# A chunked RWKV-7 scan with one multiplication by the inverse, and rotary queries projected once

## The reference, cut to what matters

```
# RWKV-7, per head of 64 (8 heads), token by token
sa    = einsum('bhvk,bhk->bhv', state, a_t)
state = state * w_t + sa[..., None] * b_t + v_t[..., None] * k_t
y_t   = einsum('bhvk,bhk->bhv', state, r_t)

# MLA: 8 heads of 64 plain and 32 rotary columns
q      = rms_norm(c_q, q_norm) @ w_uq
q_rope = [x1 * cos - x2 * sin, x2 * cos + x1 * sin]     # halves of the 32
```

## Time and profile before

| | us |
|---|---|
| median of 3 runs (1507.62 to 1509.68) | 1509.52 |
| the profiled execution | 1508.86 |
| its span in the trace | 1507.1 |

### The profile page before, as it was taken

How to read it: one execution, slowest core, us unless ns; L and a number is a source line. 1 busy time by engine, 2 the same in 40 slices (tenths; PEclk the granted TensorE clock), 3 DMA queues, 4 the chain that set the end, 5 groups by cost and what they waited for, 6 DMA issues and landing times.

```text
span 1507.1 us, 24905 instructions
## 1 busy us (share of the span) xinstructions
PE 1475.0 (98%) x9685; PEld 1218.0 (81%) x9685; DVE 1043.1 (69%) x1626; ACT 683.4 (45%) x1232; POOL 132.5 (9%) x163
## 2 busy tenths in 40 slices
PE   6999999999999999999999999999999999999998
PEld 5987888777777888887788888888888888888887
DVE  6566764578687582679865489777777757777785
ACT  7555664244433213756313246444444433333453
POOL 1013320000010001364000020000000000000000
PEclk9999999999999999999999999999999999999999
DMA  5031002722222536204446115444443699889754
GB/s 193 15 80 43 16 16 63 225 68 71 83 73 62 170 126 150 90 4 137 130 163 240 54 58 175 152 153 154 150 149 136 229 332 326 277 281 301 270 180 151
DMA packets 181115, 216.53 MB, mean 144 GB/s; under 512 B 28789, under 2 KB 115186, under 8 KB 180242
## 3 DMA queue, kind: packets, MB, share of 16 engines
q1 hardware_dynamic: 180942, 215.11, 43.5%
q10 hardware_dynamic: 68, 0.02, 0.0%
HBM read 156.20 MB, written 56.92 MB: 141 GB/s over the span
## 4 chain that ended last, share of the span: by engine, by line
PE 84%; DVE 8%; ACT 4%; issue 2%; DMA 2%; SPq 0%; ACTq 0%; DVEq 0%
PE bank L3113 20%; PE bank L3511 20%; PE bank L3575 13%; PE bank L3476 5%; PE bank L3417 4%; PE bank L3011 3%; PE bank L3023 2%; PE bank L3038 2%; PE bank L2900 2%; PE bank L2967 2%; PE bank L3048 2%; DVE down_raw L2715 1%; DVE hacc L2755 1%; PE bank L3606 1%; PE bank L2931 1%
## 5 line engine op out<-in xcount | busy, mean ns | idle before, releaser
L3113 PE MATMUL bank<-uT_hi,w_hi 128*128 128x512 f32 x432 | 170.8, 395 | 0.0
L3113 PE MATMUL bank<-uT_hi,w_lo 128*128 128x512 f32 x432 | 168.2, 389 | 0.0
L3113 PE MATMUL bank<-uT_lo,w_hi 128*128 128x512 f32 x432 | 168.2, 389 | 0.0
L3575 PE MATMUL bank<-mg_lo,mg_hi 128*128 128x512 f32 x576 | 134.8, 390 | 0.6 <-DVE mg_hi L2722 0.6
L3575 PEld LDWEIGHTS bank<-mg_lo,mg_hi 128*128 128x128 f32 x576 | 107.9, 188 | 24.2 <-DVE mg_hi L2722 1.9
L3575 PE MATMUL bank<-yh,mg_lo 128*128 128x512 f32 x384 | 118.2, 389 | 0.0
L1419 ACT ACTIVATE zbuf<-bank 128x512 f32<-128x512 f32 x54 | 32.2, 599 | 173.2 <-PE bank L3113 168.9
L1786 ACT ACTIVATE f<-f 128x512 f32<-128x512 f32 x64 | 40.5, 632 | 131.6 <-DVE f L2680 69.7
L3113 PEld LDWEIGHTS bank<-uT_hi,w_hi 128*128 128x128 f32 x432 | 81.1, 188 | 21.7 <-issue 5.2
L3113 PEld LDWEIGHTS bank<-uT_hi,w_lo 128*128 128x128 f32 x432 | 81.1, 188 | 17.4 <-issue 1.0
L3113 PEld LDWEIGHTS bank<-uT_lo,w_hi 128*128 128x128 f32 x432 | 81.1, 188 | 17.1
(11 more groups left out here) (510 smaller groups left out, 3759.2 us busy)
## 6 DMA issues: line engine op xcount, KB each, us to landing
down_raw<-in_w_ff_down SPq DMA_DIRECT2D x80, 512.0 KB, 4.9
down_raw<-f_spill SPq DMA_DIRECT2D x56, 512.0 KB, 4.8
f_spill<-x SPq DMA_DIRECT2D x80, 256.0 KB, 2.9
w_raw<-in_w_in SPq DMA_DIRECT2D x28, 512.0 KB, 4.2
sgate<-gate_spill SPq DMA_DIRECT2D x16, 512.0 KB, 4.2
up_a<-in_w_ff_up SPq DMA_DIRECT2D x16, 512.0 KB, 4.9
up_b<-in_w_ff_up SPq DMA_DIRECT2D x16, 512.0 KB, 4.1
f_spill<-f SPq DMA_DIRECT2D x32, 256.0 KB, 2.6
```

The lines of the kernel that those rows point to most:

```text
L3113: ins = nc.tensor.matmul(ps[2 * slot + g][:], st[:, slot, k, :], mv[:, k, g * HALF:(g + 1) * HALF], start=(k == 0 and m == 0), stop=(k == ...
L3575: ins = nc.tensor.matmul(ps[4 * (q % 2) + t][:], st, mv_, start=(start and w == 0 and m == 0), stop=(stop and w == 1 and m == 2))
```

## The change

**Scan.** The right side of the triangular system is now summed in PSUM: `mv` writes masked scores times values into banks 3 (even heads) and 4 (odd heads) and leaves the sums open; `right_side(n)` adds `a` times the state to them. DVE copies bank 3 and ACT bank 4 to `wv` (`x_evac`), `u_product(n)` is now the inverse times `wv`, and DVE copies the even heads and ACT the odd ones into `vu` (`u_copy`). `solve_mv`, `solve_a`, `naturals(., 2)`, `an` and `tat` are gone; `NATS` = 3 counts the naturals. `right_side` pairs the two heads' rows; `u_product` takes rows `own(m)` and writes rows `other(m)` for both heads. `y_product` of the step before is cut in two halves, placed behind `right_side(2i+1)` and `state_product(2i+1)`. ACT's and DVE's lists are written in another order, SP's loads of `lnw` and of `wo_raw` wait for other products, and `transpose_y` uses bank 0.

**Rotary queries.** `rot` is no longer projected. DVE multiplies the x output by the sine table (whose sign rows are swapped) and by the cosine table, then `stream_shuffle` rotates each group of 32 rows of the sine product by 16. There are 28 outputs instead of 32, and their order changes: x(0,0), q, q, x(0,1), q, q, x(1,0), k, k, x(1,1), k, k, then four q, four k and eight v. `uq_parts` makes two copies for each part instead of four. The subtraction that makes `fw_lo` for the first fill moves from DVE to POOL, and the banks of the v outputs are permuted.

TensorE's list in a steady step of the scan, before: from `mv(j, 0)` over the second `u_product` (L3303) to the second `solve_mv` (L3275).

The core of the diff (renamed counters, permuted tiles and the same edits at the ends of the loop are left out):

```diff
-OUTS = [o for g in range(2) for o in
-        [(kind, g, j) for j in range(2) for kind in ("x", "rot")] + [(kind, g, j) for kind in ("q", "k") for j in range(NH // 2)]]
+OUTS = [o for g in range(2) for o in [("x", g, 0), ("qk"[g], 0, 0), ("qk"[g], 0, 1), ("x", g, 1), ("qk"[g], 0, 2), ("qk"[g], 0, 3)]]
+OUTS += [(kind, 1, j) for kind in ("q", "k") for j in range(NH // 2)]
 OUTS += [("v", i // 4, i) for i in range(NT)]
 BANKS = (2, 6, 7, 4, 5, 3, 0, 1)
-V_BANKS = (2, 4, 5, 0, 1, 3, 6, 7)
+V_BANKS = (5, 3, 1, 2, 0, 6, 7, 4)
...
-                    if kind == "v" and j == 2:
-                        rest_fill(0)
                     if kind == "v" and j % 2 == 0:
                         continue
                     dve.wait_ge(s_qp, n + 1)
                     if kind == "x":
                         if 2 * g + j:
                             dve.wait_ge(s_rs, 2 * g + j)
+                        nc.vector.tensor_tensor(rp_sin[:], bank[:], sinT[:, sl], ALU.mult)
                         nc.vector.tensor_tensor(rp_cos[:], bank[:], cosT[:, sl], ALU.mult).then_inc(s_qd, 1)
-                    elif kind == "rot":
-                        nc.vector.tensor_tensor(rp_sin[:], bank[:], sinT[:, sl], ALU.mult).then_inc(s_qd, 1)
+                        dve.wait_ge(s_qd, evacuated_dve(n) - 1)
+                        nc.vector.stream_shuffle(rp_sin[:], rp_sin[:], [(r + ROPE // 2) % ROPE for r in range(ROPE)]).then_inc(s_qd, 1)
...
+                pool.wait_ge(s_wch, KD + 2)
+                nc.gpsimd.tensor_tensor(fw_lo[:], fw_raw[0][:], fw_hi[:].bitcast(F32), ALU.subtract).then_inc(s_wcl, 1)
...
+                def x_evac(n):
+                    r = own(n % 2)
+                    act.wait_ge(s_xm, n + 1)
+                    nc.scalar.activation(wv[r, 1, :], ps[4][r, 0:256], ACT.Copy).then_inc(s_xea, 1)
+
+                def u_copy(n):
+                    i, m = n // 2, n % 2
+                    act.wait_ge(s_um, n + 1)
                     if i >= 3:
                         act.wait_ge(s_ym, i - 2)
+                    u = vu[other(m), (i + 1) % 3, m, :].rearrange("p (c h v) -> p c h v", h=2, v=RH)[:, :, 1, :]
+                    nc.scalar.activation(u, ps[6][other(m), 0:256].rearrange("p (c v) -> p c v", v=RH), ACT.Copy).then_inc(s_ua2, 1)
...
+                def x_evac(n):
+                    r = own(n % 2)
+                    dve.wait_ge(s_xm, n + 1)
+                    nc.vector.tensor_copy(wv[r, 0, :], ps[3][r, 0:256]).then_inc(s_xed, 1)
+
+                def u_copy(n):
                     i, m = n // 2, n % 2
                     dve.wait_ge(s_um, n + 1)
-                    dve.wait_ge(s_tw, 2 * (i + 1))
-                    u = vu[other(m), (i + 1) % 3, m, :].rearrange("p (c h v) -> p h c v", h=2, v=RH)
-                    both = banks[other(m), 5 * 512:7 * 512].rearrange("p (h q) -> p h q", h=2)[:, :, 0:256]
-                    nc.vector.tensor_tensor(u, both.rearrange("p h (c v) -> p h c v", v=RH), u, ALU.add).then_inc(s_us, 1)
+                    if i >= 3:
...
+                                rows = own(m)
+                                ins = nc.tensor.matmul(ps[3 + h][rows, c * RH:(c + 1) * RH], mq[h][rows, i % 3, c, 0, :],
+                                                       vu[rows, (i + 1) % 3, m, (2 * c + h) * RH:(2 * c + h + 1) * RH],
+                                                       start=(c == 0), stop=False, skip_group_check=True)
+                    ins.then_inc(s_mv, 1)
+
+                def right_side(n):
                     i, m = n // 2, n % 2
+                    pe.wait_ge(s_mv, 2 * i + 2)
                     pe.wait_ge(s_st, n + 1)
+                    tok = slice(i * P + CH * m, i * P + CH * m + CH)
                     for c in range(RC):
                         for h in range(2):
                             rows = slice(64 * h, 64 * h + 64)
+                            ins = nc.tensor.matmul(ps[3 + h][own(m), c * RH:(c + 1) * RH], ar[rows, c, 0, tok],
+                                                   state[rows, n % 2, c, :], start=False, stop=True, skip_group_check=True)
+                    ins.then_inc(s_xm, 1)
+
+                def u_product(n):
+                    i, m = n // 2, n % 2
+                    pe.wait_ge(s_xed, n + 1)
+                    pe.wait_ge(s_xea, n + 1)
+                    for c in range(RC):
+                        for h in range(2):
+                            ins = nc.tensor.matmul(ps[5 + h][other(m), c * RH:(c + 1) * RH], tt[own(m), 16 * c + 2 * i + h, :],
+                                                   wv[own(m), h, c * RH:(c + 1) * RH], start=True, stop=True)
                     ins.then_inc(s_um, 1)
...
                 for i in range(-1, NT - 1):
                     j = i + 1
                     if i >= 0:
+                        right_side(2 * i)
+                    products(j, 0)
+                    if i >= 0:
                         u_product(2 * i)
-                    products(j, 0)
                     naturals(j, 1)
                     if i >= 0:
                         state_product(2 * i)
                     products(j, 1)
-                    mv(j, 0)
+                    if i >= 0:
+                        right_side(2 * i + 1)
+                    if i >= 1:
+                        y_product(i - 1, 0, 2)
                     if i >= 0:
                         u_product(2 * i + 1)
-                    naturals(j, 2)
+                    naturals(j, 3)
+                    if i >= 0:
+                        state_product(2 * i + 1)
+                    if i >= 1:
+                        y_product(i - 1, 2, RC)
                     if i >= 3:
                         transpose_y(i - 3)
                     if j == 0:
                         pe.wait_ge(s_iba, RC + RC)
                         pe.wait_ge(s_ibd, RC + RC)
-                    solve_mv(j, 0)
-                    if i >= 0:
-                        state_product(2 * i + 1)
-                    naturals(j, 3)
-                    if i >= 1:
-                        y_product(i - 1, 0, RC)
+                    mv(j, 0)
                     mv(j, 1)
-                    solve_a(j)
-                    solve_mv(j, 1)
                     if j + 1 < NT:
                         naturals(j + 1, 0)
```

More of the change, by code:

```diff
@@ L123, in evacuated_dve @@
 def evacuated_dve(n):
-    return TABLES + sum(kind != "v" or j % 2 == 1 for kind, _, j in OUTS[:n + 1])
+    return TABLES + sum(2 if kind == "x" else kind != "v" or j % 2 == 1 for kind, _, j in OUTS[:n + 1])
 FILL_UNITS = 16
@@ L2444, in _ @@
                     if i >= 0:
-                        u_add(2 * i)
+                        x_evac(2 * i)
+                        u_copy(2 * i)
                     if j < NT:
@@ L2449, in _ @@
                         state_update(2 * i)
+                    if i >= 2:
+                        y_var(i - 2)
+                    if i >= 0:
+                        x_evac(2 * i + 1)
                     if j < NT:
                         mask(j, 1)
+                    if i >= 0:
+                        u_copy(2 * i + 1)
                     if i == NT - 1:
                         o_low(0)
-                    if i >= 0:
-                        u_add(2 * i + 1)
-                    if i >= 2:
-                        y_var(i - 2)
-                    if j < NT and i >= 0:
-                        state_update(2 * i + 1)
-                    if i == NT - 1:
                         o_low(1)
@@ L2463, in _ @@
                         y_scale(i - 2)
+                    if j < NT and i >= 0:
+                        state_update(2 * i + 1)
                     if i == 1:
@@ L3221, in naturals @@
                     if i or c:
[L3222 removed]
+                        pe.wait_ge(s_nat, NATS * i + (c + 1) // 2)
+                    if c == 0 and i >= 5:
+                        pe.wait_ge(s_yt, i - 4)
                     if i == NT // 2 and c == 0:
@@ L3261, in mv @@
                             for m in range(2):
-                                rows = slice(CH * m, CH * m + CH)
-                                ins = nc.tensor.matmul(ps[3][rows, (2 * q + h) * RH:(2 * q + h + 1) * RH],
-                                                       mq[h][rows, i % 3, 2 * hs + q, 0, :],
-                                                       vu[rows, (i + 1) % 3, m, (2 * (2 * hs + q) + h) * RH:(2 * (2 * hs + q) + h + 1) * RH],
-                                                       start=True, stop=True)
@@ L3267, in mv @@
-                    ins.then_inc(s_wm, 1)
-                def solve_mv(i, hs):
-                    pe.wait_ge(s_we, 2 * i + hs + 1)
-                    for q in range(2):
-                        for h in range(2):
-                            for m in range(2):
-                                rows, v0 = slice(CH * m, CH * m + CH), (2 * q + h) * RH
```

(20 more changed lines are left out.)

150 lines of the change are left out of this document (62 added, 88 removed).

## The result

The changed kernel takes 1518.81 us (median of 4, 1515.52 to 1519.38) against 1509.31 for the kernel before (median of 4, one run more than the 1509.52 shown ahead of the prediction): 1.0062 of it, 95% interval 1.005 to 1.0074. It is 9.5 us slower; forecast were 3.2, and the range ended at 1518.0. The direction was right, and the time lies outside the range. The span of the profiled execution grew from 1507.1 to 1517.6.

The account below looks back on a forecast made before the run. TensorE's issue was taken to bound the kernel, busy 98% of the span. Rotary -4.1, scan +6.7, semaphore tests +0.4 and behind the scan +0.5 gave +3.5, forecast 1512.7 us; own range 1509.5 to 1516, stated range 1506.0 to 1518.0.

Parts of the forecast that it names:

- The rotary part: Projections to attention: four outputs fewer save 5.5 us on TensorE, of which 4.1 were taken to arrive.
- `u_product` in one quarter: Scan: 16 instructions in one array quarter take 1.13 us to the last result instead of 0.68; 7.2 us over 16 groups.
- Rival 1: Scan: u_product keeps its old pace, 7.2 us less, total 1505.5; chance 0.12.
- ACT's `x_evac` behind the copies of the values: Steady scan step: ACT copies the values first, so u_product waits 0.6 us.
- Rival 2: Scan: waits are hidden, some 1.0 us less for each of 7 steps, 1505.7 to 1507; chance 0.08.
- Step 1: Second scan step: three roundings of gup on ACT delay x_evac; 12.97 us instead of 11.12, +1.9.
- step 2: Third scan step: two more roundings, 1.29 us, make it 12.84; +1.5 with the old stall kept.
- the stall of 0.97: Issue stall in the old kernel's third scan step, 0.97 us, assumed to remain after the change.
- The end: Scan's last two chunks, with little to lay beside them: 7.56 us becomes 10.3, +2.8.
- The handovers: Scan: TensorE's extra semaphore tests before u_product and state_product, 0 to 1.6 us, taken as 0.4.
- rival 4: Scan: state's path 0.3 us dearer at each of 16 turns, +5, total 1517.5; chance 0.17.
- Behind the scan: After the scan: ACT reaches its gate copies later, between 0 and +1.5 us, taken as +0.5.

Follow-up runs that it names:

- e5: e3 with u_product's odd-head results in rows own(m) of bank 6, so two quarters are used; 1506.90 us, 0.9986 of the kernel before.
- e6: e3 with ACT's x_evac of each even chunk ahead of the copies of the values; 1510.84 us.
- e3: Changed kernel with ACT's roundings of gup in steps 1 and 2 moved behind the first copy of kb; 1514.03 us, 1.0037 of the kernel before.
- e2: Kernel before with only the scan part of the change; 1521.03 us, 1.0086 of the kernel before.
- e11: e3 with ACT's rounding of sgt ahead of the last u_copy and sg's ahead of the attention output's second rounding; 1512.27 us, 1.0023 of the kernel before.
- e4: Changed kernel with products(j, 0) issued twice in steps 1 and 2, filling part of TensorE's long waits; 1514.43 us, 1.0037 of the kernel before.
- e7: e5 and e6 together, against e3: two quarters and the earlier x_evac; 0.9992 of the kernel before.
- e12: e11 with DVE's second o_low behind y_scale; 1512.37 us, 1.0024 of the kernel before.

## Why the prediction was wrong

- **The rotary part** (-4.1): right in each of its steps to 0.2 us; 4.8 us at the first exponential, 3.8 at the scan, 3.4 in the time. What took the 1.0 was no step of the forecast: the load of `zl`, 470 us later. "Attention and what follows are bound by TensorE and move with it" was too strong, by 1 us in this execution.
- **`u_product` in one quarter** (7.2, inside the steps): shown. The forecast had 1.13 us to the last result, the trace has 1.11 to 1.14, and `e5` gets 0.43 back each time. Rival 1 is out.
- **ACT's `x_evac` behind the copies of the values** (0.6 of waiting per step): shown; 0.49 in the trace, and `e6`'s scan is 2.1 us shorter; the rest goes to what is late next (the square, in ACT's list). Rival 2 is out.
- **Step 1** (+1.9) is the step that failed, with half of step 2. The forecast had the wait and its length right (1.41 for the roundings) and priced it as a wait only, with nothing for the work behind it. The rows of before have the clock at 1.00 throughout, but they come from a TensorE that waited 1.0 us at most in the scan and 1.3 right behind it, so they could not say what 1.8 us would do. The missing 3.4 us (2.43 and 1.0) are what `e3` gets back beyond the wait. The size of the miss is partly chance: in `e2` the same step 1 lost 1.5 us less, and in the changed kernel's run of 1515.52, which lies within the range, the mean clock was 0.998 instead of 0.994. Step 2 looked nearly right in the table only because the stall of 0.97, which did not come, had been added.
- **The end** (+2.8) is the second term that failed, by nearly as much: 5.6 was measured. The walk ended it with TensorE's last products and put the gate tiles 1 us behind; ACT's list behind the last `u_copy` (a copy of `vT`, a rounding of the attention output, `sgt`, `sg`) ends it. `e11` gets 2.0 of it back. The clock fell here too, without a price: `e3` has 1.00 up to the first gate product and the same length (13.23), with a longer wait for `sg` (2.1 instead of 0.8). In nine of the eleven profiles with the new scan the clock fell for some 3.5 us in the last `y_product` or in the gate products behind it, in none of the three with the old scan; the forecast had no term for that.
- **The handovers** (0.4): the steps without a slow clock were long by 0.32 to 0.63 each, 2.7 in all with steps 1 and 2. In the steady step, 0.36 for two turns of the path, each turn took 0.18 more than the walk gave it; no run separates the semaphores from the lists in that. It is rival 4's mechanism at a little over half its price. Its 1517.5 came closest to the time, mostly for another reason.
- **Behind the scan** (+0.5): -0.3.

## What to carry to other kernels

A wait that a change puts into a busy TensorE may cost more than its length: look in a trace of the kernel for a wait of that length, and where there is none, put a slow-clock stretch into the range, as a chance and not as a fixed price. Count by quarters of the array when a group of small products is regrouped: two quarters side by side made this group 0.43 us shorter, 16 times. And when a copy joins the path of a recurrence, list what stands ahead of it on its engine in every pass of the loop, the one-time work in the first passes and behind the last too.

## What the runs showed of the hardware

- The granted clock fell after the idle time, not in it: full during 1.89 us of idleness, half for 6.9 us of the dense work behind it in the changed kernel, and for 3.5 us behind the same 1.89 in `e2`. After 1.23 us (`e4`) it fell for 3.4 us, after 1.12 and after each 0.49 of the steady steps not at all. After 2.1 us it fell in `e3`, after 2.24 at the same place in `e7` it did not.
- With equal idle times (0.50, 0.56, 0.51 in `e11` and `e12`) it fell in one execution and not in the other. The loss is no fixed price; the changed kernel's four runs spread over 3.9 us, and the fastest has the highest mean clock (0.998, the others 0.994).
- Float32 products of 64 columns in two quarters with the same rows and other columns run side by side: 16 instructions in 0.68 us, against 1.11 in one quarter.
